# Unit 9 split, unit 14 cut the plain way, four places for the weight halves, and the channel mean five products later, in a two-layer decoder trunk

## What is computed

```python
def pool_conv_layer(x, norm_g, w_in, pool_w, pool_scale, conv_w, conv_b, cn_g, cn_b, w_out):
    h = rms_norm(x, norm_g)
    proj = jnp.einsum('bsd,de->bse', h, w_in)
    a, bv, bg, z = jnp.split(proj, [A_W, A_W + B_W, A_W + 2 * B_W], axis=-1)
    pooled = multiscale_pool(a.reshape(B, S, POOL_GROUPS, POOL_CH))
    ya = jnp.einsum('bsgc,gce->bsge', pooled, pool_w).reshape(B, S, A_W) * pool_scale
    u = bv * jax.nn.sigmoid(bg)
    u = lax.conv_general_dilated(u, conv_w[:, None, :], ...) + conv_b   # causal, depthwise, 31 taps
    yb = jax.nn.silu(layer_norm(u, cn_g, cn_b))
    y = jnp.concatenate([ya, yb], axis=-1) * jax.nn.silu(z)
    return jnp.einsum('bse,ed->bsd', y, w_out)
```

## Time and profile before

| | |
|---|---|
| median of 3 runs | 331.78 us (331.74 to 331.89) |
| profiled execution | 331.88 us, its span 330.1 us |
| busy share of the span | PE 98%, DVE 78%, ACT 70%, POOL 16% |
| DMA, mean over the span | 196 GB/s |

### The profile page before, as it was taken

The page is one execution under the profiler, slowest core; times in us unless marked ns, Lnnn a source line. Parts: engine busy times, 40 slices in busy tenths (PEclk is TensorE's granted clock), DMA queues, the critical chain, the costliest instruction groups (busy, mean ns, idle before and its releaser), DMA issues.

```text
span 330.1 us, 5760 instructions
## 1 busy us (share of the span) xinstructions
PE 323.8 (98%) x2212; PEld 295.0 (89%) x2212; DVE 256.1 (78%) x475; ACT 230.4 (70%) x429; POOL 51.3 (16%) x58
## 2 busy tenths in 40 slices
PE   7999999999999999999999999999999999999995
PEld 7899999999989999998989999988887777778885
DVE  2799989999689999996886899647556787748633
ACT  4687999994999897945785457824746667576630
POOL 0050024324422310120000000005400140500000
PEclk9999999999999999999999999999999999999998
DMA  7989488979999997676639344790634323300003
GB/s 275 412 283 347 151 275 212 203 172 343 278 250 341 175 387 289 130 174 209 255 115 382 140 134 132 265 363 2 254 127 148 129 111 131 122 0 2 2 0 127
DMA packets 12842, 64.77 MB, mean 196 GB/s; under 512 B 1424, under 2 KB 1552, under 8 KB 6544
## 3 DMA queue, kind: packets, MB, share of 16 engines
q1 hardware_dynamic: 8064, 53.78, 43.7%
q0 software_dynamic: 4608, 10.49, 17.4%
q10 hardware_dynamic: 144, 0.15, 0.2%
HBM read 52.88 MB, written 1.05 MB: 163 GB/s over the span
## 4 chain that ended last, share of the span: by engine, by line
PE 87%; DMA 4%; DVE 3%; ACT 3%; issue 1%; ACTq 0%
PE bank L1060 24%; PE bank L1061 23%; PE bank L1062 23%; PE bank L1094 4%; DMA w_lo<-raw 3%; PE bank L1120 2%; PE bank L1168 2%; PE bank L1274 2%; PE bank L1301 2%; PE bank L1137 2%; PE bank L1287 2%; DMA X<-xT 1%; PE bank L1253 1%; ACT scratch L467 1%; DVE scratch L754 1%
## 5 line engine op out<-in xcount | busy, mean ns | idle before, releaser
L725 DVE TENSOR_TENSOR w_lo<-raw,w_hi 128x1024 fp32r<-128x1024 f32 x76 | 90.2, 1219 | 19.1 <-ACT w_hi L459 18.8
L1060 PE MATMUL bank<-h_hi,w_hi 128*128 128x256 f32 x304 | 86.7, 285 | 0.3 <-DMA w_lo<-raw 0.3
L459 ACT CAST w_hi<-raw 128x1024 fp32r<-128x1024 f32 x84 | 84.3, 1047 | 2.7 <-PE bank L1062 2.7
L1062 PE MATMUL bank<-h_hi,w_lo 128*128 128x256 f32 x304 | 86.0, 283 | 0.0
L1061 PE MATMUL bank<-h_lo,w_hi 128*128 128x256 f32 x304 | 86.0, 283 | 0.0
L1060 PEld LDWEIGHTS bank<-h_hi,w_hi 128*128 128x128 f32 x304 | 58.3, 192 | 0.7 <-issue 0.7
L1061 PEld LDWEIGHTS bank<-h_lo,w_hi 128*128 128x128 f32 x304 | 58.3, 192 | 0.1
L1062 PEld LDWEIGHTS bank<-h_hi,w_lo 128*128 128x128 f32 x304 | 58.3, 192 | 0.0
L843 DVE SCALAR_TENSOR_TENSOR scratch<-scratch,params 128x256 f32<-128x256 f32 x108 | 44.0, 477 | 0.2
L1060 PE MATMUL bank<-w_hi,h_hi 128*128 128x512 f32 x96 | 39.2, 408 | 0.0
L1060 PE MATMUL bank<-ya_hi,w_hi 128*128 128x256 f32 x128 | 38.1, 297 | 0.0
(11 more groups left out here) (106 smaller groups left out, 544.6 us busy)
## 6 DMA issues: line engine op xcount, KB each, us to landing
raw<-w SPq DMA_DIRECT2D x49, 1024.0 KB, 6.4
side_v<-side_ring POOLq DMA_DIRECT2D x24, 256.0 KB, 8.2
w_lo<-raw POOLq DMA_DIRECT2D x8, 512.0 KB, 7.9
X<-xT SPq DMA_DIRECT2D x2, 512.0 KB, 5.2
out<-X SPq DMA_DIRECT2D x4, 256.0 KB, 2.7
consts<-const SPq DMA_DIRECT2D x1, 290.0 KB, 13.6
params<-vec ACTq DMA_DIRECT2D x1, 149.0 KB, 4.9
```

Of the source, the lines that this page charges most:

```text
L459: nc.scalar.copy(halves(w_hi, cut_slot(n), half), halves(raw, n % RAW, half)).then_inc(hi_cut, 1)
L725: nc.vector.tensor_tensor(halves(w_lo, cut_slot(n), half), halves(raw, n % RAW, half), halves(w_hi, cut_slot(n), half).bitcast(F32), ALU.s ...
L1060: nc.tensor.matmul(dst, wh, ah, start=start, stop=False, skip_group_check=True)
L1062: return nc.tensor.matmul(dst, wl, ah, start=False, stop=stop, skip_group_check=True)
```

## The change

Unit 9 becomes a plain split, where it was native. Unit 14 becomes a plain split, where it was an added one. Up to `FOUR`, which is `ZA[1]` and so unit 18, the halves rotate over all four places; units 19 and 20 follow the old rule of three. Unit 22 waits for the last unit up to 18 that used the fourth place, which is 18 itself. Two statements move in the loops of ACT and DVE, and `MEAN_AT` and `SUM2_AT` name later places.

```diff
-NATIVE = frozenset((0, 9, 13, 16, 21, 23, 25))
-EARLY_ADDED = (10, 14)
+NATIVE = frozenset((0, 13, 16, 21, 23, 25))
+EARLY_ADDED = (10,)
 ADDED = EARLY_ADDED + (22, 24)
 SPARE = 22
+FOUR, SLOT_ORDER = ZA[1], (3, 2, 0, 1)
...
     if n == SPARE or n >= Z1[0]:
         return (n - Z1[0]) % 4 if n >= Z1[0] else CUT - 1
-    return (cut_index(n) - (n > SPARE) - cut_index(Z1[0]) + 1) % 3
+    if n > FOUR:
+        return (cut_index(n) - (n > SPARE) - cut_index(Z1[0]) + 1) % 3
+    return SLOT_ORDER[(cut_index(FOUR) - cut_index(n)) % 4]
...
     if n == SPARE:
-        return released(PW)
+        return released(max(m for m in CUTS if m <= FOUR and cut_slot(m) == CUT - 1))
...
-MEAN_AT = 2, 0, 1
-SUM2_AT = 2, 1, 6
+MEAN_AT = 2, 0, 6
+SUM2_AT = 3, 0, 4
...
                 for pair, item in side_items(n):
                     side_product(pair, item)
+                if n + 3 in EARLY_ADDED:
+                    cut_hi(n + 3)
                 if n in A:
...
-                if n + 3 in EARLY_ADDED:
-                    cut_hi(n + 3)
                 if n == PW:
...
-                if m in A:
+                if m in A and n + 2 not in EARLY_ADDED:
                     window_sums(m - A[0])
...
                 taps(n)
+                if m in A and n + 2 in EARLY_ADDED:
+                    window_sums(m - A[0])
```

## The result

The changed kernel takes 337.04 us, the median of six runs (334.97 to 337.63), where the one before takes 331.77. The ratio is 1.0147, with an interval of 1.0125 to 1.0169: slower, by 5.3 us where 3.2 were forecast, and 0.4 us above the range. The profiled execution took 336.97 us, with a span of 334.9. The span runs from the first instruction to the last.

What follows compares the result with a forecast made beforehand. The prediction took TensorE, busy 98% of the span, as the bound, with a rigid 20.24 us chain from mean to unit 26. Unit 26 starting 3.15 us later gave 331.88 + 3.15 = 335.0 us; range 333.2 to 336.6.

Steps and rivals of the forecast that it cites:

- Unit 9 and unit 14 on TensorE: Unit 9's split gains 1.16 us, unit 14's 0.3 us wait goes; TensorE reaches the pool maps 1.46 us earlier.
- Moved statements and places at nothing: The statements moved on ACT and DVE and the four places for halves change no timing: zero cost.
- DVE ready for the cut of unit 19 at 114.8, ACT not before 115.4: DVE would be ready at 114.8, but ACT's cut behind the pool-map scalings lets it start only at 115.4.
- DVE from there to the mean, +6.1 us: From unit 19's cut to the end of the additions DVE takes 6.1 us more than 30.9, ending at 152.4.
- the 1.4 us: DVE's new wait at the head of slot 19 for ACT's copy and two scalings: +1.4 us.
- without the 1.4 us wait alone: Case within the 12% rival that DVE is in time: only the slot 19 wait doesn't come, giving 333.6.
- The mean's place and the way to unit 26: TensorE reaches the later mean at 150.17, waits 2.2 us; the rigid 20.24 us chain starts unit 26 3.15 us later.
- Unit 10's DMAs at nothing: Unit 10's adding DMAs, issued later, take 9.0 us and land in time for TensorE: cost 0, bounds 0 to 2.1 us.
- rival 2: Unit 10 is late as well: TensorE waits up to 2.1 us at 68.6, total 335.3 to 337.1; 15%.
- the clock: Rival: waits lower TensorE to 1.2 GHz for 3.9 us of products behind the mean, adding 3.9: 338.9; 2%.

Runs made afterwards that it cites:

- e4: Changed kernel with the last 14 single taps of DVE's slot 21 done on 8 of 256 columns: 334.22 us, ratio 1.0074.
- e9: Changed kernel with unit 9 native again, the plan then having 18 single taps in slot 21: 333.52 us, ratio 1.0051.
- e10: Changed kernel with unit 10 first on ACT and POOL, and slot 19 opening with DVE's own taps before ACT's product: 336.74 us, ratio 1.0125.
- e11: Changed kernel, unit 10 first, plan shares 1.0 (46 taps on ACT's products), e10's slot 19 order, mean and sum of squares at the old places: 332.44 us.
- e2: Kernel before the change, with only the changed kernel's later places for the mean and the sum of squares: 334.01 us, ratio 1.0058.
- e1: Changed kernel with five extra matmuls, result thrown away, on TensorE just ahead of its wait for the mean: 336.04 us, ratio 1.0122.
- e5: e1 with SP holding the load of unit 13 until unit 9 has ended, as before the change: 335.00 us, ratio 1.0096.
- e6: e1 with unit 10's cut ahead of slot 7's side products on ACT, its adding DMAs ahead of theirs on POOL: 335.13 us, ratio 1.01.
- e3: Changed kernel with the mean and the sum of squares back at the places of before: 338.88 us, ratio 1.0201.
- e12: e6 without the five extra matmuls, so the changed kernel with only unit 10 first on ACT and POOL: 337.41 us, ratio 1.016.

## Why the prediction was wrong

*Unit 9 and unit 14 on TensorE.* Right. TensorE reaches the pool maps 1.3 us earlier (104.66 + 6.92 = 111.58, forecast 111.46), and the wait at unit 14 is gone.

*Moved statements and places at nothing.* Right. The order of instructions shows the statements inert for unit 10. No wait on a place is new in the trace: ACT waits once for TensorE ahead of a high half, 2.7 us behind unit 26, as it did before.

*DVE ready for the cut of unit 19 at 114.8, ACT not before 115.4.* Right in what decides: ACT let DVE start at 115.60. DVE was ready at 115.60 - 1.52 = 114.08, 0.7 us before the forecast, which costs and wins nothing.

*DVE from there to the mean, +6.1 us.* Right to 0.1: 152.58 - 115.60 = 36.98, where 30.92 + 6.1 = 37.0. As terms, single taps, the five products and the wait in slot 19 came out as 11.2, 3.1 and 1.57. e4, with 14 of the 28 taps made short, confirms that the tail holds the mean, and e9, with 18 taps in it, fits. But the 1.4 us were mis-read in one way: e10 and e11 show that the order in slot 19 is not their cause. With the order changed DVE waits for ACT at the next places. That ACT's work from the high half of ya to slot 20 is one chain, which DVE meets at one place or another, is my reading of these rows; no run shortened that work by itself. The lower bound of 333.6 for the case "without the 1.4 us wait alone" was not reached by e10's order.

*The mean's place and the way to unit 26.* Right at a full clock: e2 shows the way to be rigid with 2.19 us for 2.16, and with work in place of the wait it takes 20.5 us (e1, e5, e6) for 20.24.

*Unit 10's DMAs at nothing.* Right in the changed kernel's profiled execution, where they took 9.2 and 9.6 us, wrong in others. I took 9.0 us from the row of the same transfer, which had no load beside it. e5 against e1 shows the load of unit 13 to lengthen it by 3.4 to 4.2 us in those executions. In the changed kernel the first half landed at 59.43 + 9.2 = 68.6, with nothing to spare. In e1, e3 and e4 TensorE waited 0.2, 0.9 and 0.7 us there. This is rival 2, and it had 15%.

**The step that failed** is the clock. The prediction gave it 2% and put the sum at a full clock throughout, on the ground that "no row shows it either way". The runs show that a standstill of 2.5 us ahead of the mean is followed by 3.4 us at 1.2 GHz in most executions: four of the changed kernel's six runs, at 336.97 to 337.63, have a mean clock of 0.993 to 0.995, and the other two, at 334.97 and 335.95, have 0.998 and 0.999. The first of these two is the forecast of 335.0; the other is 1.0 us above it, as its span is, which a late unit 10 would explain, but it was not profiled. e1 against the changed kernel and e6 against e12 show the cause: with work in place of the standstill the clock stays, and where unit 10 is in time as well, the time is 335.1. With the clock kept up and unit 10 late the median is within the range (e1, 336.04); with unit 10 first and no matmuls it is above it (e12, 337.41), though 0.8 us of that lie outside the span. The size was off as well, in the other direction: 1.7 us of lost clock in the profiled execution, of which 1.35 reach unit 26 (against e1), where the rival had 3.9. The Trainium skill (TensorE: Matmul & The Clock Gate, Part 1) said as much as that an idle TensorE falls back to half rate; the trace agrees, at 0.51.

The reasoning error is this. I worked out a wait of 2.2 us on an engine that had never stood still for over 1.0 us, knew that nothing in the trace told what follows on it, and still gave a full clock 98%. Where the trace is silent and the wait is forecast, the two cases deserved something near even chances, and the range should have reached 335.0 + 1.7 and a part of unit 10's lateness, 337 or 338.

## What to carry to other kernels

A saving on the engine that bounds the kernel is worth what the helping engines can follow: here 1.16 us of TensorE's work and a wait of 0.3 were bought with 4.6 us on a DVE that had hardly a gap, and the plan put that work where it could not hide, just ahead of the mean. A wait that is new to TensorE has two prices, its length and what it does to the clock behind it, and filling it with matmuls that nobody reads can be the cheaper wait. A load that is freed to start earlier will start beside something: look at which transfer with a deadline is in flight there.

## What the runs showed of the hardware

- After TensorE stood still for 2.2 to 2.5 us the granted clock fell to half in most executions, and stayed at full in others of the same kernel (by the mean clock, four of six fell in the changed kernel and in e10, four of four in e12). In the four profiled executions in which it fell (the changed kernel, e3, e10, e12) it was at half for 3.4 us each time, also after the 4.6 us of e3. From the mean to unit 26 they took 21.8 to 21.9 us, where e1, e5 and e6 took 20.5. After waits of 1.0 to 1.5 us the clock stayed full (e2, e5, e6, e11).
- The clock is still full during the standstill. In the changed kernel it is 0.99 from 150.28 to 152.73, when TensorE has work again, and 0.51 behind it. In e12 TensorE has work again at 153.10, and the fall comes 0.7 us later (granted clock 1.00 from 153.0 to 153.5, 0.79 to 154.0, then 0.50). So the work that follows pays.
- An adding DMA of 512 KB took 5.1 and 6.4 us without a load of 1 MB beside it and 9.3 and 9.8 us with one on SP's queue, issued at the same times, with other adding DMAs beside it both times (e5, e1). With the load beside it the time differs between executions: 6.9 and 8.2 us in e6, 10.5 and 10.9 in e12, in the same order.
